# Expert stage in unrounded fp32 products on column strips of the array: 64 stationary columns for neighbouring token groups, 32 for the rest

## What is computed

```python
SEQ, D_MODEL, N_EXPERTS, TOP_K, D_EXPERT = 256, 1024, 8, 2, 3584
def swiglu(h, w_gate, w_up, w_down):
    return (jax.nn.silu(h @ w_gate) * (h @ w_up)) @ w_down

def moe_swiglu(h, w_router, w_gate, w_up, w_down):
    logits = (h @ w_router).astype(jnp.float32)
    top_val, top_idx = lax.top_k(logits, TOP_K)
    top_w = jax.nn.softmax(top_val, axis=-1)
    combine = jnp.sum(jax.nn.one_hot(top_idx, N_EXPERTS, dtype=jnp.float32) * top_w[..., None], axis=-2)
    out = jnp.zeros(h.shape, jnp.float32)
    for e in range(N_EXPERTS):
        y = swiglu(h, w_gate[e], w_up[e], w_down[e]).astype(jnp.float32)
        out = out + combine[..., e:e + 1] * y
    return out.astype(h.dtype)
```

## Time and profile before

| | us |
|---|---|
| median of 3 runs | 1709.31 (1706.87 to 1709.41) |
| the profiled execution | 1710.03 |
| its span, first to last instruction | 1708.2 |
| of this before the first gather, at 695.0 | 695 |
| from 701.5 to 1692.0, the experts' loop | 990.5 |

### The profile page before, as it was taken

How to read it: one execution, slowest core, us unless ns; L and a number is a source line. 1 busy time by engine, 2 the same in 40 slices (tenths; PEclk the granted TensorE clock), 3 DMA queues, 4 the chain that set the end, 5 groups by cost and what they waited for, 6 DMA issues and landing times.

```text
span 1708.2 us, 23843 instructions
## 1 busy us (share of the span) xinstructions
PE 1658.3 (97%) x7872; PEld 1368.8 (80%) x7872; DVE 1404.9 (82%) x1533; ACT 1221.0 (71%) x1439; POOL 49.1 (3%) x33
## 2 busy tenths in 40 slices
PE   7998999999999899999999999999999999999996
PEld 5876788888887778788888888888888888888885
DVE  5877675565777767899899899998998998998997
ACT  5677645444567764778788787887887887788785
POOL 0130000000013000000000000000000000000000
PEclk9999999999999999999999999999999999999999
DMA  9434265555543435599899899898998998998993
GB/s 368 163 132 148 101 246 199 190 189 182 200 148 124 148 105 195 197 370 378 324 372 372 327 373 369 326 370 340 361 372 340 351 378 330 363 375 328 369 374 132
DMA packets 66120, 470.96 MB, mean 276 GB/s; under 512 B 7312, under 2 KB 7568, under 8 KB 9744
## 3 DMA queue, kind: packets, MB, share of 16 engines
q1 hardware_dynamic: 64768, 462.97, 71.6%
q0 software_dynamic: 864, 6.29, 1.0%
q10 hardware_dynamic: 432, 0.96, 0.2%
HBM read 469.15 MB, written 1.05 MB: 275 GB/s over the span
## 4 chain that ended last, share of the span: by engine, by line
PE 79%; DVE 9%; ACT 7%; issue 4%; DMA 1%; SPq 0%; DVEq 0%; ACTq 0%
PE bank L501 16%; PE bank L503 16%; PE bank L502 16%; PE mid L501 8%; PE mid L503 8%; PE mid L502 8%; DVE w_lo L496 3%; ACT w_hi L489 2%; PE turn L1161 2%; PE turn L1203 1%; DMA raw<-in_stream 1%; PE mid L1051 1%; DVE xT L1458 1%; DVE root L1462 1%; DVE gy L1476 1%
## 5 line engine op out<-in xcount | busy, mean ns | idle before, releaser
L496 DVE TENSOR_TENSOR w_lo<-raw,w_hi 128x1024 fp32r<-128x1024 f32 x877 | 1066.8, 1232 | 230.3 <-ACT w_hi L489 190.1
L489 ACT ACTIVATE w_hi<-raw 128x1024 fp32r<-128x1024 f32 x877 | 924.4, 1060 | 313.7 <-PE bank L503 188.8
L501 PE MATMUL bank<-w_hi,g_hi 128*128 128x512 f32 x896 | 355.2, 396 | 0.5
L503 PE MATMUL bank<-w_hi,g_lo 128*128 128x512 f32 x896 | 350.0, 391 | 0.0
L502 PE MATMUL bank<-w_lo,g_hi 128*128 128x512 f32 x896 | 349.6, 390 | 0.0
L501 PE MATMUL bank<-w_hi,a_hi 128*128 128x512 f32 (+1 forms) x608 | 242.3, 399 | 14.1 <-DVE w_lo L496 12.0
L503 PE MATMUL bank<-w_hi,a_lo 128*128 128x512 f32 (+1 forms) x608 | 234.8, 386 | 0.0
L502 PE MATMUL bank<-w_lo,a_hi 128*128 128x512 f32 (+1 forms) x608 | 234.6, 386 | 0.0
L501 PEld LDWEIGHTS bank<-w_hi,g_hi 128*128 128x128 f32 x896 | 168.7, 188 | 37.5 <-DVE w_lo L496 3.4
L503 PEld LDWEIGHTS bank<-w_hi,g_lo 128*128 128x128 f32 x896 | 168.6, 188 | 36.2
L502 PEld LDWEIGHTS bank<-w_lo,g_hi 128*128 128x128 f32 x896 | 168.8, 188 | 33.4
(11 more groups left out here) (217 smaller groups left out, 1510.3 us busy)
## 6 DMA issues: line engine op xcount, KB each, us to landing
raw<-in_stream SPq DMA_DIRECT2D x438, 1024.0 KB, 4.8
wg<-in_gates POOLq DMA_DIRECT2D x2, 2048.0 KB, 10.6
gain<-in_norms POOLq DMA_DIRECT2D x4, 512.0 KB, 4.2
x<-in_x SPq DMA_DIRECT2D x2, 512.0 KB, 5.9
raw<-in_stream SPq DMA_DIRECT2D x2, 512.0 KB, 6.8
out_x<-xn SPq DMA_DIRECT2D x4, 256.0 KB, 2.0
const<-in_consts ACTq DMA_DIRECT2D x1, 752.0 KB, 13.2
gain<-in_norms SPq DMA_DIRECT2D x2, 256.0 KB, 7.0
```

The source lines that it names most:

```text
L489: nc.scalar.activation(w_hi[:, h % H, :], raw[:, part % R, lo:lo + HALF], ACT.Copy).then_inc(hi_ready, 1)
L496: nc.vector.tensor_tensor(w_lo[:, h % H, :], raw[:, part % R, lo:lo + HALF], w_hi[:, h % H, :].bitcast(F32), ALU.subtract).then_inc(lo_rea ...
L501: nc.tensor.matmul(out_, s_hi, wh, start=start, stop=False)
L503: return nc.tensor.matmul(out_, s_lo, wh, start=False, stop=stop)
```

## The change

The expert stage no longer splits anything but the output. `gT`, `hT` and the weights in `raw` are plain float32. An expert's tokens are limited to 96 (`CAP`), three groups of 32, and go over the array's columns in strips of 32: where four blocks of weights (two of gate, two of up, or two column halves of two rows of down) meet three groups of tokens, that is twelve strips, three times the array's width. A product takes one block of weights as the moving operand and one strip, or two neighbouring strips where two groups of tokens meet the same weights, as the stationary one. With more than 96 tokens on one expert, two further passes over all experts would follow (before: one, above 128).

The weights are packed anew so that a part holds the four blocks of the same rows; the parts stay 42 an expert and 1 MB each. A quad is one such group of hidden columns: three of 4 x 512 and one of 4 x 256. Quads use two sets of three PSUM banks by turns (`early`, `late`). The down products go to `turn`. SP now loads a part when PE has used the one in its slot (`used`), as ACT and DVE don't read weights any more.

```diff
...
 DSTEPS = F_DENSE // CB
-ESTEPS = F_EXP // CB
-E_PARTS = 6 * ESTEPS
-NPASS_TOKENS = P
+STRIP = 32
+GROUPS_E = 3
+CAP = STRIP * GROUPS_E
+QUADS = (512, 512, 512, 256)
 
 
 def dense_order():
...
-        out += [("gate", c), ("up", c)]
-        if 0 < c < ESTEPS - 2:
-            out += [("down", c - 1)]
-    return out + [("down", c) for c in range(ESTEPS - 3, ESTEPS)]
-
+    for q, w in enumerate(QUADS):
+        out += [("in", q, kt) for kt in range(0, KT, CB // w)]
+    for q, w in enumerate(QUADS):
+        out += [("down", q, k) for k in range(w // P)]
+    return out
+
+
+E_ORDER = expert_order()
+E_PARTS = len(E_ORDER)
+N_IN = E_ORDER.index(("down", 0, 0))
+AFTER_QUAD = [E_ORDER.index(("in", q + 1, 0)) for q in range(len(QUADS) - 1)] + [N_IN]
+TILE_AT = [sum(QUADS[:q]) // P for q in range(len(QUADS))]
+AT_COMBINE = [2 + m for m in range(4)]
+AT_HID = [i + 2 for i in AFTER_QUAD]
+AT_SLOT = N_IN + 3
+AT_GATHER = [N_IN + 6, N_IN + 8]
+E_TURNS = 4 + 2 * (len(QUADS) - 1)
 
...
             hT_lo = [keep(f"hT_lo{i}", [P, 4, T], F32R, m) for i in range(2)]
         with ExitStack() as m:
-            xn_hi = keep("xn_hi", [P, TB, D], F32R, m)
-            xn_lo = keep("xn_lo", [P, TB, D], F32R, m)
-            g_hi = keep("g_hi", [P, KT, P], F32R, m)
-            g_lo = keep("g_lo", [P, KT, P], F32R, m)
-            eh = [keep(f"eh{i}", [P, CB], into=m) for i in range(2)]
-            eT_hi = [keep(f"eT_hi{i}", [P, 4, P], F32R, m) for i in range(2)]
-            eT_lo = [keep(f"eT_lo{i}", [P, 4, P], F32R, m) for i in range(2)]
+            xs = keep("xs", [P, TB, D], into=m)
+            gT = keep("gT", [P, KT, CAP], into=m)
+            eh = [keep(f"eh{i}", [P, 2, CB], into=m) for i in range(2)]
+            hT = keep("hT", [P, sum(QUADS) // P, 2 * CAP], into=m)
             y_hi = keep("y_hi", [P, D], F32R, m)
             y_lo = keep("y_lo", [P, D], F32R, m)
-            sel = keep("sel", [P, TB, P], F32R, m)
+            yt = keep("yt", [P, CB], into=m)
+            sel = keep("sel", [P, TB, CAP], into=m)
             selT = keep("selT", [P, T], F32R, m)
+            keep("sel_end", [P, 64], into=m)
...
+        early = [bank[0][:, :], bank[1][:, :], bank[2][:, :]]
+        late = [bank[3][:, :], mid[:, 0, :], mid[:, 1, :]]
...
+        def part_landed(eng, pas, i, e):
+
+            n = STATIC_PARTS + pas * E_LAST + i
+            eng.wait_ge(landed[n % R], 16 * (n // R + 1) + e * (16 * E_PARTS // R))
 
...
 
+            def expert_loads(u0):
+
+                with sp.Fori(0, EXPERTS - 1) as e:
+                    for i in range(E_PARTS):
+                        sp.wait_ge(used, u0 + i + 1 + e * E_PARTS)
+                        load((STATIC_PARTS + i) % R, STATIC_PARTS + R + i + e * E_PARTS)
+                for i in range(E_LAST - E_PARTS, E_LAST - R):
+                    sp.wait_ge(used, u0 + i + 1)
...
+                    for q, w in enumerate(QUADS):
+                        place = (early, late)[q % 2]
+                        act.wait_ge(used, u0 + AFTER_QUAD[q] + e * E_PARTS)
+                        nc.scalar.activation(eh[q % 2][:, 0, 0:w], place[0][:, 0:w],
+                                             ACT.Silu).then_inc(e_silu, 1)
+                        nc.scalar.activation(eh[q % 2][2 * STRIP:P, 1, 0:w], place[2][0:2 * STRIP, 0:w],
+                                             ACT.Silu).then_inc(e_silu, 1)
...
+            def gather(j):
+
                 for k in range(4):
                     kt = 4 * j + k
-                    for i, (src, b) in enumerate([(s_, b) for b in range(TB) for s_ in (xn_hi, xn_lo)]):
-                        ins = nc.tensor.matmul(t_[:, k * P:(k + 1) * P], src[:, b, kt * P:(kt + 1) * P],
-                                               sel[:, b, :], start=i == 0, stop=i == 2 * TB - 1)
-                ins.then_inc(turned, 1)
-
-            def combine(idx, i, e):
+                    for b in range(TB):
+                        ins = nc.tensor.matmul(early[j][:, k * CAP:(k + 1) * CAP], xs[:, b, kt * P:(kt + 1) * P],
+                                               sel[:, b, :], start=b == 0, stop=b == TB - 1)
+                ins.then_inc(g_full, 1)
+
...
+            def strips(s_, n):
+                return slice(STRIP * s_, STRIP * (s_ + n))
+
+            def turn_hidden(q, top, rest, full):
+
+                for k in range(QUADS[q] // P):
+                    ins = nc.tensor.transpose(top[:, k * P:(k + 1) * P],
+                                              eh[q % 2][:, 0, k * P:(k + 1) * P], ident)
+                ins.then_inc(full, 1)
+                half = slice(2 * STRIP, P)
+                for k in range(QUADS[q] // P):
+                    ins = nc.tensor.transpose(rest[:, k * 2 * STRIP:(k + 1) * 2 * STRIP],
+                                              eh[q % 2][half, 1, k * P:(k + 1) * P], ident[half, half])
+                ins.then_inc(full, 1)
 
             def experts(pas):
...
-                                          start=c == 0 and hh == 0, stop=c == ESTEPS - 1 and hh == 3)
+                                    pe.wait_ge(sel_ready, TB * (c0 + 2) + e * TB)
+                                    pe.wait_ge(hT_top, q0 + len(QUADS) + e * len(QUADS))
+                                    pe.wait_ge(hT_rest, q0 + len(QUADS) + e * len(QUADS))
+                                gather(j)
+                        part_landed(pe, pas, i, e)
+                        w_ = raw[:, (STATIC_PARTS + i) % R, :]
+                        if what == "in":
+                            place = (early, late)[q % 2]
+                            w = QUADS[q]
+                            if (q, k0) == (0, 0):
+                                pe.wait_ge(g_ready, 2 * (c0 + 1) + e * 2)
+                                pe.wait_ge(selT_ready, pas * EXPERTS + 1 + e)
+                            for kt in range(k0, k0 + CB // w):
+                                o = (kt - k0) * 4 * w
+                                g0, g1, u0, u1 = (w_[:, o + c * w:o + (c + 1) * w] for c in range(4))
+                                for bank_, tiles in zip(place, (((g0, 0, 0, 2), (g0, 2, 2, 1), (g1, 3, 0, 1)),
+                                                                ((u0, 0, 0, 2), (u0, 2, 2, 1), (u1, 3, 0, 1)),
+                                                                ((g1, 0, 1, 2), (u1, 2, 1, 2)))):
+                                    for w_c, s_, t_, n in tiles:
+                                        ins = nc.tensor.matmul(bank_[strips(s_, n), 0:w], gT[:, kt, strips(t_, n)],
+                                                               w_c, start=kt == 0, stop=kt == KT - 1)
                         else:
-                            o_ = bank[2 * (c % 2) + (what == "up")]
-                            if what == "gate" and c == 0 and hh % 2 == 0:
-                                read_out(t0 + hh // 2, e)
-                            pe.wait_ge(lo_ready, h + 1 + e * E_HALVES)
-                            for k in range(2):
-                                kt = 2 * hh + k
-                                ins = mm3(o_[:, :], g_hi[:, kt, :], g_lo[:, kt, :],
-                                          w_hi[:, h % H, xslice(k)], w_lo[:, h % H, xslice(k)],
-                                          start=kt == 0, stop=kt == KT - 1)
+                            if (q, k0) == (0, 0):
+                                pe.wait_ge(hT_top, q0 + len(QUADS) - 1 + e * len(QUADS))
+                                pe.wait_ge(hT_rest, q0 + len(QUADS) - 1 + e * len(QUADS))
+                            if (q, k0) == (len(QUADS) - 1, 0):
+                                pe.wait_ge(hT_top, q0 + len(QUADS) + e * len(QUADS))
+                                pe.wait_ge(hT_rest, q0 + len(QUADS) + e * len(QUADS))
+                            first, last = i == N_IN, i == E_PARTS - 1
+                            h_ = hT[:, TILE_AT[q] + k0, :]
+                            for c in range(2):
+                                n0, n1 = (w_[:, c * D + n * CB:c * D + (n + 1) * CB] for n in range(2))
+                                for w_c, s_, t_, n in ((n0, 0, 0, 2), (n0, 2, 2, 1), (n1, 3, 2, 1)):
+                                    nc.tensor.matmul(turn[0][strips(s_, n), :], h_[:, c * CAP + STRIP * t_:
+                                                                                   c * CAP + STRIP * (t_ + n)], w_c,
+                                                     start=first and c == 0, stop=last and c == 1)
+                            for c in range(2):
+                                n1 = w_[:, c * D + CB:(c + 1) * D]
+                                ins = nc.tensor.matmul(turn[1][strips(2 * c, 2), :], h_[:, c * CAP:c * CAP + 2 * STRIP],
+                                                       n1, start=first, stop=last)
                         ins.then_inc(used, 1)
-                pe.wait_ge(y_ready, 2 + 2 * (EXPERTS + 1) * (pas + 1))
...
```

(51 more changed lines are left out.)

309 lines of the change are left out of this document (151 added, 158 removed).

## The result

The changed kernel takes 2456.49 us, median of 4 runs (2454.57 to 2458.34), against 1708.94 before: ratio 1.4375, 95% interval 1.4356 to 1.4393. The forecast was 2458.

What follows compares the result with a forecast made beforehand. PE was taken to bound the kernel, DMA not far behind. The 1708.2 us span plus 8 x 93.9 for the experts, less 3 around the loop, gave 2456, with 1.8 around execution 2458; 8-in-10 range 1740 to 2650.

Steps and rivals of the forecast that it cites:

- the splits worth nothing: Expert loop: 672 of 877 halves lose their splitting, 712 us of ACT and 828 of DVE, gaining nothing by itself.
- A plain float32 product of 512 columns costs 0.86, and strips of one width run together: Expert parts: a product is two records of 0.43 us; two strips of 64 columns run at the same time.
- The switch, 0.14: Expert parts: PE empties when column width changes between 64 and 32, 0.14 us each, four switches (0.56 us) in an ordinary part.
- My upper bound: Expert parts: every change between 64 and 32 empties PE and 64s never run beside 32s; 4.86 us a part.
- the rival in which only overlapping widths wait: Expert parts: widths that don't overlap run together, those that do empty; 132.5 us an expert, 1777 total; chance 0.15.
- The sum: Whole kernel: 217.6 us an expert, 93.9 more than before, eight times, less 3 around the loop; 2458 total.
- The 26 switches of full-width work at 0.17: Each expert: combines, turnings, slots' transposes and gather halves between strips cost 26 width changes, 4.4 us.
- Around the loop I took 3 us off: Head and tail: first gather at 96 columns, without `g_lo` and first splits, saves 3 us; tail keeps its chain.
- the part of 5.3 at 0.25 a switch: Forecast's dear case: at 0.25 us a switch a part takes 5.3 us and the total is 2600.
- The loads hidden: Expert loop: loads run ahead by four parts, so their landing is hidden; DMA's share falls to about 0.54.
- The floor of the loads: Expert loop: 44.0 MB an expert at 376 GB/s take at least 117.1 us, 2.79 a part.
- everything side by side: Expert parts: no emptying between 64 and 32; 119.6 us an expert, 1674 total, nothing under 1654 possible; chance 0.14.

Runs made afterwards that it cites:

- the kernel of 32s: Changed kernel with each product of 64 columns made two of 32, so the array has one width in a part: 1701.66 us, 0.9962 of before.
- the mirrored one: Changed kernel with each part's products ordered by width, 64s first, and up's 64-column product moved to strips 2 and 3: 1964.01 us.
- taking 103 away: Changed kernel with the same products of a part ordered by width, the 64-column ones first, then the 32-column ones: 2343.21 us.
- the kernel of 32s, written out: All products as strips of 32 columns, with PE's loop over the experts written out, so without a branch back: 1678.17 us, 0.9818 of before.
- the grouped kernel: Strips of 32, PE's loop written out, and full-width work (combines, gather halves, slots' transposes) put together at fewer places: 1669.96 us, 0.9777 of before.
- the kernel with groups left out: Strips of 32, PE's loop written out, two of three strip groups not computed in two of eight row blocks of each quad: 1586.45 us.
- the kernel of 32s with work left out: Strips of 32, PE looped, only the first strip of each group computed in two of eight row blocks of a quad: 1700.67 us.
- two experts: Changed kernel with PE's loop running four times over two experts in place of eight times over one: 2455.45 us.

## Why the prediction was right

- **The bound.** PE before and after, and the splits worth nothing: shown by DVE's and ACT's 12.4 us an expert beside PE's 217.2, and by an expert's time in the kernels above, which followed PE's turns and switches.
- **A plain float32 product of 512 columns costs 0.86, and strips of one width run together.** Shown by 0.43 between groups of four loads in the kernel of 32s, and by the pairs of 64s in the mirrored one.
- **The switch, 0.14.** Taken from full width to 64, where the trace had it, and carried over to 64 and 32, where it had nothing. Measured 0.136 by taking 103 away, and 0.12 to 0.14 between groups. Together with the half-empty array (25 and 72 us an expert) this was the whole loss. My upper bound was the right one; the rival in which only overlapping widths wait is refuted by the loads, as a 32 waits for a 64 beside it, and by 217 where it gave 132. What the Trainium skill states in TensorEngine Tiling (Array Packing), Key Properties, that a change of tiling mode drains the engine, holds here between 64 and 32 columns too.
- **The sum.** 217.6 forecast for an expert, 217.17 measured. Two small errors stand in it, and luck has them cancel. An ordinary part was 4.83 (down parts' last pairs start at 1296.62, 1301.45, 1306.28) and not 4.86, some 1.3 us less over the 42. The gather's records stand 0.11 apart at 96 columns too, where I had scaled them down to 0.083, 0.9 more; this is also why the kernel of 32s, written out, has 120.2 and not 119.6. The 26 switches of full-width work at 0.17 were about right (0.16 in the grouped kernel). Around the loop I took 3 us off and 2.8 went, but 1.0 of it lies before the first gather, where nothing changed: that start varies from 692.4 to 697.6 in the profiles of these kernels. So the total within 2 us is closer than the working deserves.
- **Slips that changed nothing.** By the same sum, the part of 5.3 at 0.25 a switch gives a total of some 2620, not 2600. In the records of L1101 the first one on each of the two strips has 323 ns, not one alone; the reading stays.
- **The loads hidden.** The share was to be 0.54 and is 0.55.
- **Where it was off.** The floor of the loads, 117.1 us an expert, came from the 376 GB/s of a stretch with share 0.98. That stretch was not at its limit: the same loads took 108.8 us in the kernel with groups left out. The forecast itself didn't rest on it, but the rival "everything side by side" did, with its bar at 1654. And that rival's 1674 for three full turns a part was out of reach of a looped kernel for a reason that I had not thought of, the branch: 1702 with it and 1678 without. What is left to 1674 is mostly the gather.

## What to carry to other kernels

Before merging strips of the array to save instructions, write down the turns: products of unlike column width did not run beside each other here, and every change of width costs about 0.14 us here, so a few more instructions of one width were better than fewer of two. Judge a packed schedule by the fullest strip and by the order of widths, not by the number of products. If an engine's loop body is made longer, look at what the engine does at the loop's end, and ask how long the work queued there lasts.

## What the hardware showed that I had not expected

- PE's branch back to the loop's start took 0.22 us with a body of 1251 or 1640 instructions (PE's records from one branch to the next, before and in the changed kernel), 4.4 to 4.7 with 2088 (the kernel of 32s with work left out), 4.4 to 6.0 with 2376 (all 32s) and 3.6 to 3.9 with 3278 (two experts). That length is the cause is shown by the pair with the same work; between 1640 and 2088 no body was run. The short bodies were fetched once, the long ones in every round.
- The loads ran at 404 GB/s over 859 us. A share of 0.98 with 376 GB/s elsewhere was no ceiling, so the share of busy DMA engines can't be scaled up to one.
- Two strips of 32 columns in place of one of 64 cost nothing, though they have twice the load and matmul pairs: a part of 24 pairs took 2.58 us, three turns.
